# Four lightly loaded experts of a hierarchical MoE as one unit of four, in an order found on the chip

## The reference, cut to what matters

```python
def hier_moe(h, w_rg, w_re, w1, w3, w2):
    xt = h.reshape(B * L, D)
    pg = jax.nn.softmax((xt @ w_rg).astype(jnp.float32), axis=-1)
    p_grp, g_idx = lax.top_k(pg, 1)
    ...
    pe_top, e_idx = lax.top_k(jax.nn.softmax(le, axis=-1), 2)
    pe_top = pe_top / jnp.sum(pe_top, axis=-1, keepdims=True)
    expert = g_idx * MOE_PER_GROUP + e_idx
    weight = p_grp * pe_top
    combine = jnp.sum(jax.nn.one_hot(expert, MOE_EXPERTS, dtype=jnp.float32) * weight[..., None], axis=1)
    hid = jax.nn.silu(jnp.einsum('nd,xdf->nxf', xt, w1)) * jnp.einsum('nd,xdf->nxf', xt, w3)
    y = jnp.einsum('nxf,xfd->nd', hid * combine[..., None].astype(hid.dtype), w2)
```

## Time and profile before

| | |
|---|---|
| median of 3 runs | 1402.55 us (1402.51 to 1402.69) |
| the profiled execution's own time | 1400.19 us |
| its span, first to last instruction | 1398.0 us |
| mean granted PE clock | 0.995 of full speed |
| PE busy | 1343.8 us, 96% |
| DVE busy, ACT busy | 473.5 us, 286.2 us |
| bytes moved | 554.37 MB, mean 397 GB/s |

### The profile page before, as it was taken

How to read it: one execution, slowest core, us unless ns; L and a number is a source line. 1 busy time by engine, 2 the same in 40 slices (tenths; PEclk the granted TensorE clock), 3 DMA queues, 4 the chain that set the end, 5 groups by cost and what they waited for, 6 DMA issues and landing times.

```text
span 1398.0 us, 17305 instructions
## 1 busy us (share of the span) xinstructions
PE 1343.8 (96%) x7140; PEld 743.5 (53%) x7140; DVE 473.5 (34%) x1067; ACT 286.2 (20%) x514; POOL 32.1 (2%) x30
## 2 busy tenths in 40 slices
PE   9999999999988899999999988999999999999996
PEld 4786585444434688775444424854444356444433
DVE  3787514111114797624112113141111144111113
ACT  3311024111103122224111103241111035111102
POOL 0001310000000000010000000100000000000000
PEclk9999999999999999999999999999999999999999
DMA  9997999999999995789999999889999998999995
GB/s 384 420 398 271 421 420 414 428 427 427 428 428 418 422 406 227 264 357 407 428 426 428 428 428 419 349 364 414 427 428 428 427 419 359 407 426 428 427 427 210
DMA packets 55654, 554.37 MB, mean 397 GB/s; under 512 B 6097, under 2 KB 8081, under 8 KB 9233
## 3 DMA queue, kind: packets, MB, share of 16 engines
q1 hardware_dynamic: 53792, 551.19, 94.7%
q10 hardware_dynamic: 1778, 2.01, 0.4%
HBM read 551.08 MB, written 2.10 MB: 396 GB/s over the span
## 4 chain that ended last, share of the span: by engine, by line
PE 79%; DMA 16%; DVE 2%; ACT 1%; SPq 1%; issue 0%; POOL 0%; DVEq 0%; POOLq 0%
PE bank L773 26%; PE bank L719 14%; PE bank L797 13%; DMA ring<-in_moe_w 10%; PE bank L738 5%; DMA ring<-in_w_ada 4%; PE bank L756 4%; PE bank L679 3%; PE bank L565 2%; DMA ring<-in_hy_w_in 2%; PE bank L693 2%; PE bank L549 1%; PE bank L1022 1%; PE bank L906 1%; PE bank L629 1%; PE bank L623 1%
## 5 line engine op out<-in xcount | busy, mean ns | idle before, releaser
L773 PE MATMUL bank<-ring,hT 128*64 128x512 f32 x1024 | 225.3, 594 | 0.0
L773 PE MATMUL bank<-ring,arena 128*64 128x512 f32 x896 | 199.6, 595 | 22.3 <-DMA ring<-in_moe_w 22.3
L797 PE MATMUL bank<-ring,arena 128*64 128x512 f32 x896 | 198.5, 595 | 0.0
L1533 DVE TENSOR_TENSOR rows<-rows,bank 128x512 f32<-128x512 f32 x32 | 22.0, 688 | 456.5 <-PE bank L773 456.5
L773 PEld LDWEIGHTS bank<-ring,hT 128*64 128x64 f32 x1024 | 72.1, 137 | 139.3 <-issue 137.6
L773 PEld LDWEIGHTS bank<-ring,arena 128*64 128x64 f32 x896 | 63.8, 137 | 150.7 <-issue 128.3
L797 PEld LDWEIGHTS bank<-ring,arena 128*64 128x64 f32 x896 | 61.7, 137 | 116.9 <-issue 115.2
L1552 DVE SCALAR_TENSOR_TENSOR yv_rest<-bank,arena,yv_big 128x512 fp32r<-128x512 f32 x64 | 48.0, 750 | 199.9 <-ACT yv_big L1221 199.9
L719 PE MATMUL bank<-hT,ring 128*128 128x256 f32 x512 | 112.0, 380 | 0.3 <-DMA ring<-in_hy_w_in 0.3
L719 PEld LDWEIGHTS bank<-hT,ring 128*128 128x128 f32 x512 | 96.6, 190 | 15.1 <-issue 2.2
L1221 ACT ACTIVATE yv_big<-bank,arena 128x512 fp32r<-128x512 f32 x64 | 44.0, 688 | 281.0 <-PE bank L797 281.0
(11 more groups left out here) (227 smaller groups left out, 1375.8 us busy)
## 6 DMA issues: line engine op xcount, KB each, us to landing
ring<-in_moe_w SPq DMA_DIRECT2D x152, 2048.0 KB, 18.5
ring<-in_w_ada SPq DMA_DIRECT2D x96, 1024.0 KB, 14.8
ring<-in_moe_w SPq DMA_DIRECT2D x48, 1024.0 KB, 23.6
arena<-in_moe_w SPq DMA_DIRECT2D x16, 1024.0 KB, 14.6
arena<-in_moe_w SPq DMA_DIRECT2D x8, 2048.0 KB, 9.7
ring<-in_hy_w_in SPq DMA_DIRECT2D x12, 1024.0 KB, 27.3
ring<-in_hy_w_out SPq DMA_DIRECT2D x4, 1024.0 KB, 14.0
ring<-in_gla_w_v SPq DMA_DIRECT2D x4, 1024.0 KB, 26.2
```

Of the source, the lines that this page charges most:

```text
L773: last = mm(bank[4 + kind][SLOTS * e:SLOTS * e + SLOTS, :], x[:, k, at:at + SLOTS], w[:, kk, e, :], start=k == 0, stop=k == KD - 1)
L797: last = mm(bank[6 + q // 2][SLOTS * e:SLOTS * e + SLOTS, :], hidT[:, f, SLOTS * e:SLOTS * e + SLOTS], w[:, ff, e, :], start=f == 0, stop= ...
L1533: tt(sil[:], sil[:], bank[5][:], ALU.mult).then_inc(s(pre + "hid_ready"), 1)
```

## The change

- Experts 0, 1, 8 and 9 stay in pairs 0 and 1. The other twelve are ordered by their number of tokens, largest first, by a new function on DVE, `order_experts`. It also orders `rank` and `comb` (into `rank0` and `comb0`) and writes the experts' numbers to `order`. Where one of the last four has more than 32 tokens, a further round is asked for.
- Pairs 2 to 5 take the ordered experts two by two. The last four run as one unit (`QUAD`) with 32 slots for each expert. There are seven units a layer (UNITS) in place of eight pairs.
- In L773 and L797 the four experts of that unit take a quarter each of PE's columns.
- A slab now belongs to one expert: half of its rows for one kind. All come as transfers of 1 MB, and for units 2 and up the address comes from a register that SP loads from `order` after `order_known`.
- Semaphores of the experts' steps count halves (two a unit) in place of quarters.
- The ring position is no longer made even.

```diff
+FIXED, ORDERED = 2, EXPERTS - 4
+QUAD = PAIRS - 2
+UNITS = QUAD + 1
+QUAD_SLOTS = 32
...
-        experts = [("moe", i, p, kind, q) for p in range(PAIRS) for kind in range(3) for q in range(SLABS)
+        experts = [("moe", i, p, kind, q) for p in range(QUAD) for kind in range(3) for q in range(SLABS)
                    if p or kind < 2]
+        experts += [("moe", i, p, kind, 2 * h + e) for kind in range(3) for h in range(2) for p in (QUAD, QUAD + 1)
+                    for e in range(2)]
...
-                at += at % 2
...
-        def expert_slab(n, q):
-            return a["moe_w"][bass.ds(n, 1)][:, :, SLAB * (q % 2):SLAB * (q % 2) + SLAB].rearrange("o p n -> p (o n)")
+        def expert_slab(kind, h, n):
+            return a["moe_w"][bass.ds(LAYERS * EXPERTS * (2 * kind + h) + n, 1)].rearrange("o p n -> p (o n)")
...
+                if what[0] == "moe" and what[2] >= FIXED and what[3:] == (0, 0):
+                    i, p = what[1:3]
+                    sp.wait_ge(s("order_known"), i + 1)
+                    for e in range(2):
+                        n = (PAIRS - FIXED) * e + p - FIXED
+                        expert[p, e] = sp.value_load(order[0:1, n:n + 1], min_val=EXPERTS * i, max_val=EXPERTS * i + EXPERTS - 1)
                 if homed(what):
                     _, i, p, kind, q = what
-                    if q % 2:
-                        sp.wait_ge(s("y_mm"), primed(SLABS * PAIRS * i + q + 1))
-                        sp.dma_start(home_pair(i, q // 2), a["moe_w"][6 * (PAIRS * i + p) + 2 * kind + q // 2]) \
-                            .then_inc(s(f"homed{q // 2}"), 16)
+                    sp.wait_ge(s("y_mm"), primed(2 * UNITS * i + q // 2 + 1))
+                    sp.dma_start(first_w2[i][q], expert_slab(kind, q // 2, expert[p, q % 2])).then_inc(s(f"homed{q // 2}"), 16)
                     continue
...
-                if in_halves(what):
-                    _, i, p, kind, q = what
-                    if q % 2:
-                        sp.dma_start(ring_all[:, SLAB * (slot - 1):SLAB * (slot + 1)],
-                                     a["moe_w"][6 * (PAIRS * i + p) + 2 * kind + q // 2]) \
-                            .then_inc(s(f"full{slot - 1}"), 16)
-                    continue
                 if what[0] == "moe":
                     _, i, p, kind, q = what
-                    src = expert_slab(6 * (PAIRS * i + p) + 2 * kind + q // 2, q)
+                    n = EXPERTS * i + PAIRS * (q % 2) + p if p < FIXED else expert[p, q % 2]
+                    src = expert_slab(kind, q // 2, n)
...
-            def experts_in(pre, n, kind, x, j, weights, ready):
+            def columns(j, quad=False):
+
+                if quad:
+                    return [(P * e + SLOTS * jj, QUAD_SLOTS) for jj in range(2) for e in range(2)]
+                return [(P * e + SLOTS * j, SLOTS) for e in range(2)]
+
+            def experts_in(pre, n, kind, x, cols, weights, ready):
+
+                for h in range(2):
+                    ws = weights(kind, h)
+                    for kk in range(4):
+                        k = 4 * h + kk
+                        if kk % 2 == 0:
+                            ready(k // 2)
+                        for o, (at, m) in enumerate(cols):
+                            last = mm(bank[4 + kind][m * o:m * o + m, :], x[:, k, at:at + m], ws[o][:, kk, :],
+                                      start=k == 0, stop=k == KD - 1)
                     last.then_inc(s(pre + USED[kind]), 1)
...
-            def experts_out(pre, n, weights, ready):
+            def experts_out(pre, n, cols, weights, ready):
                 pe.wait_ge(s(pre + "hidT_ready"), primed(n + 1))
+                for h in range(2):
+                    ws = weights(2, h)
+                    ready(h)
+                    for f in range(4):
+                        for o, (_, m) in enumerate(cols):
+                            last = mm(bank[6 + h][m * o:m * o + m, :], hidT[:, f, m * o:m * o + m], ws[o][:, f, :],
+                                      start=f == 0, stop=f == 3)
                     last.then_inc(s(pre + "y_mm"), 1)
...
+            def order_experts(i):
+
+                N, each = ORDERED, [P, ORDERED, 2, PAIRS - FIXED]
+                chain(v.tensor_copy(two(o_key12), later(o_key)))
+                chain(tt(o_cmp, o_key12.unsqueeze(1).broadcast_to([P, N, N]), o_key12.unsqueeze(2).broadcast_to([P, N, N]),
+                         ALU.is_ge))
+                chain(v.reduce_sum(o_pos, o_cmp, AX.X))
+                place = iota[:, 0:N].rearrange("p (n e) -> p e n", e=2).unsqueeze(3).broadcast_to([P, 2, PAIRS - FIXED, N])
+                chain(tt(o_hot.rearrange("p (e n) x -> p e n x", e=2), place,
+                         o_pos.unsqueeze(1).unsqueeze(1).broadcast_to([P, 2, PAIRS - FIXED, N]), ALU.is_equal))
+
+                def ordered(out, values):
+                    chain(tt(o_tmp.rearrange("p s (e n) -> p s e n", e=2), o_hot.rearrange("p s (e n) -> p s e n", e=2),
+                             later(values).unsqueeze(1).broadcast_to(each), ALU.mult))
+                    chain(v.reduce_sum(out, o_tmp.rearrange("p (e n) x -> p e n x", e=2), AX.X))
+
+                ordered(two(o_id), iota[:, 0:EXPERTS])
+                ts(order[0:1, :], o_id[0:1, :], EXPERTS * i - 1.0, None, ALU.add).then_inc(s("order_known"), 1)
+                for values, out in ((rank, rank0), (comb, comb0)):
+                    for g in range(G):
+                        ordered(later(out[:, g]), values[:, g])
+                chain(ts(o_quad, o_pos, 2.0 * QUAD - 2 * FIXED + 0.5, float(SLOTS * QUAD_SLOTS), ALU.is_gt, ALU.mult))
+                for g in range(G):
+                    stt(later(rank[:, g]), two(o_quad), 1.0 / SLOTS, later(rank[:, g]), ALU.mult, ALU.add)
+                chain(tt(later(o_key), later(o_key), two(o_quad), ALU.add))
+                chain(v.reduce_max(r_mx, o_key, AX.X))
...
-                v.reduce_max(r_mx, bank[4][:, 32:48], AX.X)
+                stt(o_key, bank[4][:, 32:48], float(SLOTS), iota[:, 0:EXPERTS], ALU.mult, ALU.subtract)
...
+                order_experts(i)
                 for j in range(3):
-                    chain(ts(r_rd[:, j:j + 1], r_mx, float(SLOTS * (j + 1)), None, ALU.is_gt))
+                    chain(ts(r_rd[:, j:j + 1], r_mx, float(SLOTS * SLOTS * (j + 1)), None, ALU.is_gt))
```

More of the change, by code:

```diff
@@ L190, in build @@
             continue
[L191 to L194, removed]
+        fills[slot] += 1
+        where[what] = slot, slot, fills[slot]
     ctx = ExitStack()
@@ L230, in build @@
         over = sb("over", [1, 2], I32)
+        order = sb("order", [1, ORDERED], I32)
         bank = [ctx.enter_context(nc.psum_tensor(f"bank{i}", [P, 512], F32)) for i in range(8)]
@@ L441, in _ @@
             sp.dma_start(vec[:], a["vec"]).then_inc(s("vec_loaded"), 16)
-            last = {}
+            last, expert = {}, {}
             for what, slot, nth in stream:
@@ L762, in scatter @@
                     last.then_inc(s(pre + "scattered"), 1)
-            def experts_in(pre, n, kind, x, j, weights, ready):
-                for q in range(SLABS):
-                    w = weights(kind, q).rearrange("p k (e n) -> p k e n", e=2)
-                    ready(q)
-                    for kk in range(2):
-                        k = 2 * q + kk
-                        for e in range(2):
-                            at = P * e + SLOTS * j
-                            last = mm(bank[4 + kind][SLOTS * e:SLOTS * e + SLOTS, :], x[:, k, at:at + SLOTS],
-                                      w[:, kk, e, :], start=k == 0, stop=k == KD - 1)
+            def columns(j, quad=False):
[12 more added lines that the diff above has]
+                                      start=k == 0, stop=k == KD - 1)
                     last.then_inc(s(pre + USED[kind]), 1)
@@ L781, in hidden_rows, with slot_weights @@
                 last.then_inc(s(pre + "hidT_mm"), 1)
-            def slot_weights(pre, n, j):
+            def slot_weights(pre, n, j, quad=False):
                 for g in range(G):
-                    last = tr(bank[5][:, g * P:g * P + P], selw[:, j, g].rearrange("p e n -> p (e n)"), ident)
+                    rows_of = selq[:, g].rearrange("p x n -> p (x n)") if quad else \
+                        selw[:, j, g].rearrange("p e n -> p (e n)")
+                    last = tr(bank[5][:, g * P:g * P + P], rows_of, ident)
                 last.then_inc(s(pre + "selT_mm"), 1)
-            def experts_out(pre, n, weights, ready):
+            def experts_out(pre, n, cols, weights, ready):
                 pe.wait_ge(s(pre + "hidT_ready"), primed(n + 1))
-                for q in range(SLABS):
-                    w = weights(2, q).rearrange("p f (e n) -> p f e n", e=2)
-                    if q % 2 == 0:
-                        ready(q // 2)
-                    for ff in range(2):
-                        f = 2 * (q % 2) + ff
-                        for e in range(2):
```

(21 more changed lines are left out.)

114 lines of the change are left out of this document (64 added, 50 removed).

## The result

| | before | after |
|---|---|---|
| median | 1402.53 us (1399.03 to 1402.69, 4 runs) | 1432.04 us (1430.88 to 1433.85, 4 runs) |
| ratio | | 1.0213, 95% interval 1.0199 to 1.0228 |
| the profiled execution's own time | 1400.19 us | 1433.85 us |
| its span | 1398.0 us | 1431.7 us |
| mean granted PE clock | 0.995 | 0.953 |

The change makes the kernel slower by 29.5 us, 2.1%. The forecast was 1438, in a range of 1409 to 1449. No further round ran.

What follows compares the result with a forecast made beforehand. The prediction took weight transfers, not PE, to set each MoE layer's end. Late first pair 14.8, rate 11.7 and layer end 10.4 summed to 36.9 us more, giving 1438 us, range 1409 to 1449.

Steps and rivals of the forecast that it cites:

- The removed matmuls are worth 0: Last experts of each layer: the merged unit removes some 23.6 us of PE work where PE waits for transfers; value 0.
- 85 us less PE busy: Sign expected in the changed profile: PE busy down by some 85 us while the span gets longer.
- The late first pair: Layers 0 to 2: ordering on DVE delays ada_rows, PE idles 4.5 us and loses clock; 14.8 us after slack.
- The rate: MoE weight transfers: all at 1 MB move 421 GB/s instead of 428; 2.9 us a layer, 11.7 us in all.
- The end of the layer: Last unit's halves: PE idles 6.3 us between them, last step some 6 us at clock 0.5; 10.4 us in all.
- Register loads and the padding: SP's two loads per pair of experts hide behind queued transfers; dropping the ring's even padding gains nothing; 0 each.
- The sum: Whole kernel: 14.8 + 11.7 + 10.4 = 36.9 us on the profiled 1400.19 us, 1437.1; 1439.5 from the median, taken as 1438.

Runs made afterwards that it cites:

- pairs again: Kernel after with the last four experts as two pairs of 64 slots again; ordering, register addresses and 1 MB transfers stay: 1427.13 us, ratio 1.0184.
- rows_first: Kernel after with the copy of the adaLN result put ahead of the expert ordering on DVE: 1416.69 us, ratio 1.0107.
- pairs_rows: Kernel after with eight pairs in place of the unit of four and the adaLN copy ahead of the ordering: 1409.07 us, ratio 1.0048.
- warm_tail: Kernel after with a filler, six matmuls of ones into a free bank, between the unit of four's two w2 halves: 1428.11 us, ratio 1.0190.

## Why the prediction was right, step by step

The medians as a staircase: 1402 for the kernel before; 1406.7 with 1 MB transfers; 1409.1 with the ordering, the register addresses and halves; 1416.7 with the unit of four; 1432.0 with the copy behind the ordering.

The steps were measured in this order and in different sets of runs; another order gives other steps (the unit costs 4.9 or 7.6 us, the copy's place 15.3 or 18.1).

- **The removed matmuls are worth 0**: right. PE is busy for 46.7 us less, and its waits for expert weights grew by 70.8. With pairs again the kernel was faster. My figure of 85 us less PE busy was wrong: I did not count that the unit's matmuls are recorded longer at the lower clock. Its 24 halves take 124.6 us in all, where 24 times 3.64 would be 87.4; these 37.3 us are nearly all of the gap.
- **The late first pair, 14.8 us**: right; moving the copy gave 15.3. Its parts: the ordering 5.48 us (5.5 forecast), the idle 4.44 (4.5), and the homed issue later than the layer's routing by 7.9, 6.3 and 7.7 us in layers 0 to 2 (7.2). The routing was late by 0.9, 8.7 and 15.7 us there, by the first DVE reduce of each. The clock's share was not the same 2.7 us each time: after the idle it was back at 1.00 at about 241.2, 664.4 and 958.0, so half rate cost some 3.1, 1.6 and 3.0 us.
- **The rate, 11.7 us**: the rate was right, 421 against 428. The size was off for the edit by itself: it cost 5.3. From the homed issue to the last h3 group of layer 3, 68 slabs, it took 170.5 us before (1199.08 to 1369.60) and 174.3 with pairs of 1 MB slabs:

```profile
1222.13 4.29 SPq L481 DMA_DIRECT2D arena<-in_moe_w  x4
```

```profile
1396.42 3.65 PE L769 MATMUL bank<-ring,arena 128*64 128x512 f32 x16 [1.32 <-DMA ring<-in_moe_w]
```

In layers 0 to 2 it is 173.0 us with pairs, and 170.9 in layer 2 before. So up to the last gate it takes 2.2 us longer in layer 2 and 3.8 in layer 3 with the slower rate; I had reckoned 2.9 for 72 slabs. What I missed is that single slabs also let PE start nearer to the last landing, where the code waits for them one by one.
- **The end of the layer, 10.4 us**: the mechanism was right, its size too high. In layer 3 the end moved by 3.7 us against the stop of the transfers, where I had 2.6: the clock took 2.3 (5.92 less 3.64), and the rest is that a half starts 2.8 us after the reckoned stop and not 1.4, as I had read from the last h3 step. For all four layers the fair comparison is with the pairs at the same edits, from the first homed issue to the last expert matmul. The unit takes 1.9, 2.8, 1.6 and 2.2 us more than pairs, 8.5 in all; with the copy ahead of the ordering (rows_first against pairs_rows) it is 1.3, 3.4, 1.6 and 2.2, again 8.5. That is the term as measured, against 10.4. In the medians the unit costs 7.6 us with the copy ahead and only 4.9 with it behind. The difference arises in the mixer of layer 1: with pairs and the copy behind, the kernel leads by 2.6 us at the end of layer 0 and lies 1.2 behind at the homed issue of layer 1, since PE waits there for w_ada, gla_w_q and an adaLN copy, 7.8 us in all (0.89, 1.16 and 5.73), where the kernel after waits 3.7.
- **Register loads and the padding, 0**: not contradicted. No cost of the loads shows in layers 0 to 2; by the medians they and all else that the kernel with pairs and the copy first adds to 1 MB transfers come to about 2 us. The padding was not tried by itself.
- **The sum.** 36.9 us on the profiled execution, of which I took back 1.4 for the next mixer. By the profiles it was 33.7. The mixer gave back 2.8 after layer 0, the unit cost 8.5 and not 10.4, and 0.9 came from outside. By the medians it was 29.5, because the profiled execution of before lay 2.3 below its median and that of after 1.8 above. Set against the steps in the medians, the rate was 6.4 too high and the end 2.8, while about 2.3 stood at nothing and the late pair was 0.5 too low. So part of the closeness is that errors offset each other; the order of the parts and their mechanisms are as forecast.

The forecast rested on one reading: that the chain changes from PE to a transfer before the last two pairs are done. PE's 96% busy and 79% of the chain said nothing of that. The place was read a little wrong, though. The 26.5 us from 782.10 are a transfer's whole way from issue to landing, and PE works through most of it; 782.10 is in the sixth pair. PE first waits for a slab at the seventh pair's h3, for 0.96 us:

```profile
808.71 3.65 PE L773 MATMUL bank<-ring,arena 128*64 128x512 f32 x16 [0.96 <-DMA ring<-in_moe_w]
```

That is still ahead of the pass that the change removes, so the value of 0 stands.

The trace also agrees with the rule of the Trainium skill that was weighed there (TensorE: Matmul & The Clock Gate, HAM oscillation): all 15 halves of the unit that stood behind a wait longer than their own 3.64 us ran at the lower level for a part of their time, and the filler took the last one's away. It does not say all. Of the nine halves behind shorter waits six took 3.64 us (waits of 0.97 to 1.86 us) and three ran partly at the lower level too (1.99, 2.28 and 3.24 us).

## What to carry to other kernels

Before taking work off the busiest engine, look at which wait ends last at the place where that work lies; here work removed behind a transfer only made waits, and most of the matmuls behind them ran in part at the lower clock. An instruction put into a queue costs what stands behind it: here 5.5 us of small DVE work delayed a copy that PE was waiting for in three layers, and moving that copy gave back half of the loss. Where a ring of buffers feeds PE, measure at the one transfer that waits for a fixed point how long it takes to land; what it takes over the empty-queue time is the slack, and where that is 0 the queue's order is worth changing.

## What was not expected of the hardware

- The last half of a unit started 2.8 us behind the reckoned stop of transfers (1408.0 to 1410.80), while the last h3 step before had started 1.4 us behind the time reckoned back from the stop at 2.45 us a slab. The longer thinning out at the end, 2.0 us behind the reckoned stop in place of 1.0, would account for 1.0 of the 1.4 us between them. That is reasoned from the stretches and not tried, and why it is longer is open.
- An idle of 2.0 us was enough for the lower clock in the unit: the half at 1148.97 of layer 2 followed an idle of 1.99 us and took 5.34 us. But the clock fell only once the half had begun, as it did in two more of the 24 (1158.92 and 1400.88). These are stretches inside the first half of w2 in layer 3, which starts at 1400.88:

```profile
1400.50:1401.50 1.00, 0.62 (x8) 0.34 (x12) 0.00 (x0) 0.00 (x0) 0.00 (x0) 1.00 1.02 426
...
1402.50:1403.50 1.00, 1.00 (x9) 0.32 (x5) 0.00 (x0) 0.00 (x0) 0.00 (x0) 0.50 1.02 426
```

  In the earlier trace rows a stretch of 2 us without matmuls left the clock at 1.00, and in pairs_rows a wait of 2.53 us did (835.96, 3.65 us at 1.00). So the length of the idle by itself does not tell in which case the clock falls.
- In one kernel the runs spread by 8 us (warm_tail, 1424.31 to 1432.81), where the others spread by 0.6 to 6.3.
